# Two transformer blocks on one core: four edits inside the layers of the first block

## The chip, the core and the metric

The kernel runs on one core of a Trainium2 chip. A core has five engines with instruction streams of their own: TensorE (PE in the profile; its weight loads are PEld), VectorE (DVE), ScalarE (ACT), GpSimd (POOL) and SyncE (SP). They are ordered among themselves by semaphores alone, and every order in this kernel is written out by hand. SP and ACT issue DMAs, each on a queue of its own; both queues are served by the same 16 DMA engines. The metric is device time in microseconds of one execution. All times below are in microseconds unless marked ns.

## What is computed

The reference runs `first_block` (two layers) and then `second_block` (a feed-forward part, a hybrid mixer, a second feed-forward part, a norm) on a 512 x 1024 activation in f32. The change lies in the two layers. One layer is, cut to what matters:

```
h = rms_norm(x, norm_g) * (1 + scale) + shift          # scale, shift, gate from c @ w_ada
gq, gk, gv, glr, gz, dq, dk, dv, dz = split(h @ w_in)   # glr has 16 columns, the rank
gq, gk, gv = split(silu(causal_conv([gq, gk, gv])))
log_a = log_sigmoid(glr @ w_gk + b_gk) / 16
k_dec = gk * exp(b_end - cumsum(log_a))                 # per chunk of 64 tokens
u[n]  = k_dec[n].T @ gv[n]                              # outer products, 8 chunks
state = a[n] * state + u[n]; o[n] = gq[n] @ state       # 4 heads, 64 x 128 each
o_gla  = rms_norm(o) * gla_norm_g * silu(gz)
o_diff = rms_norm(attention difference) * diff_norm_g * (1 - lam_init) * silu(dz)
x = x + gate * (concat(o_gla, o_diff) @ w_out)
```

## The kernel before

**Weights.** A layer's weights pass through in 18 units of 128 x 2048 (`L_CONV` 4, `L_K` 2, `L_Q` 2, `L_V` 2, `L_Z` 4, `L_OUT` 4). SP loads a unit into `raw` (L460), ACT rounds it to `wh` (L539, `take_high`), GpSimd takes the remainder `wl = raw - wh` (L496). Two buffers alternate, by the parity of the unit. The activation is split alike into `xh` and `xl` (in the output units `mix_h` and `mix_l`), and PE forms each product as three matmuls, `wh*xh`, `wh*xl` and `wl*xh` (L880 to L882, `products`; for token blocks L909 to L911). PE waits for `w_ready` before it starts a unit and for `banks_free` (its PSUM banks have been emptied, or claimed again) before it writes.

**The order inside a layer.** `layer_order` makes one list of stages that all engines follow. The weight units up to z are cut into quarters, `("part", stage, j, p)`, 56 of them, and `put(n, stage)` places a smaller piece of work behind quarter n. The pieces which the change touches: `lr` (n = 3), the 16 rank columns `glr`, as 8 `products` of 128 x 512; `gate` (n = 6), `glr @ w_gk + b_gk`, in which a row of ones in `glr` carries the bias; `outer` (n = 25 to 32), the outer product of one chunk of 64 tokens per call. PE makes the outer products (L1113), DVE turns them into `states` (L1647 and L1649), and `read_out` (n = 27, 29, 31, 33; L1128) multiplies by the states. A chunk's 64 tokens lie on partitions 0 to 63 or 64 to 127, by its parity, and its outer product goes to PSUM bank 4 or 5.

**The last z unit and the first two output units.** When PE has finished the last quarter of z, ACT's list is: a root and a Silu of earlier z columns, then `take_high` for the second output unit (L539), then the Silu of the last z bank out of PSUM (L645), which releases `banks_free`. PE's list is: `claim` and `chunk_ready` for both output units, then `first_out(0, 0)` and `first_out(0, 1)` (24 matmuls of 128 x 512 with the GLA half), `turn_output(4)` and `(5)` (L1056), `first_out(1, 0)`, `turn_output(6)` and `(7)`, `first_out(1, 1)`.

**The start.** SP issues x, eight 1 MB tiles of `w_ada` and two weight units. ACT makes the squares of x and then issues the small loads (`small_loads`, L513 to L523), and only behind those stands the root for the first norm (L596). DVE turns the root into a diagonal (L1383, L1384), PE spreads it (L1001), and behind that on PE stand the `w_ada` tiles 2 to 7 (L968), whose sums give the scale and shift that the first matmuls' input needs. `o_g` holds the four output norm weights (two layers, two branches) as columns of 128 partitions; DVE multiplies two of them by `1 - lam_init` (L1533).

Of the kernel before, what the change touches and what calls it, by code (L numbers as in the profile page):

```python
# [25 lines left out]
F32 = mybir.dt.float32  # L26
# [5 lines left out]
P = 128  # L32
D = 1024
S = 512
# [43 lines left out]
def layer_order():  # L78
# [24 lines left out]
    for c in range(NCH):  # L103
        put(25 + c, "outer", c)
# [64 lines left out]
def build(nc, ins, out):  # L169
    ctx = ExitStack()  # L170
    with ctx:  # L171
# [56 lines left out]
        o_g = sb("o_g", [P, LAYERS, 2])  # L228
        c_wide = sb("c_wide", [P, KT, 32])
        wgk = sb("wgk", [RANK + 1, LAYERS, GLA_QK])  # L230
        glr = sb("glr", [32, S])
# [49 lines left out]
        wr_h = at("wr_h", [P, KT, P], F32R, at_p)  # L281
        wr_l = at("wr_l", [P, KT, P], F32R, at_p + 4096)
# [80 lines left out]
        glr_copied = sem("glr_copied")  # L363
        conv_done = sem("conv_done")
# [80 lines left out]
        N_SMALL = 16 * (len(small) + 3 + LAYERS)  # L445
# [63 lines left out]
        def _(act):  # L509

            def small_loads():
# [7 lines left out]
                act.dma_start(o_g[:], ins["o_g"].rearrange("o (l a d) -> (o d) l a", l=LAYERS, a=2), allow_slow_non_contiguous=True  # L519
                              ).then_inc(small_in, 16)  # L520
                act.dma_start(wgk[0:RANK], ins["w_gk"]).then_inc(small_in, 16)
                for l in range(LAYERS):
                    act.dma_start(wgk[RANK:RANK + 1, l], ins["b_gk"][l:l + 1]).then_inc(small_in, 16)  # L523
# [101 lines left out]
            for l in range(LAYERS):  # L625
# [3 lines left out]
                def empty(stage, j, t):  # L629
# [4 lines left out]
                    if t:  # L634
                        take_high(unit + 2)
                    bank = ps[:, t]
                    func = ACT.Silu if (stage, j) == ("z", L_Z - 1) else ACT.Copy
# [7 lines left out]
                    nc.scalar.activation(dst, bank, func).then_inc(banks_free[u], 1)  # L645

# [34 lines left out]
                for stage, *at_ in ORDER:  # L681
# [194 lines left out]
        def _(pe):  # L876
# [132 lines left out]
            for l in range(LAYERS):  # L1009
# [125 lines left out]
                for stage, *at_ in ORDER:  # L1135
# [14 lines left out]
                    elif stage == "lr":  # L1150

                        pe.wait_ge(lr_w, l + 1)
                        for k in range(KT):
                            last = products(ps[:, 4], (wr_h[:, k], wr_l[:, k]), (xh[:, k], xl[:, k]),
                                            k == 0, k == KT - 1)
                        last.then_inc(glr_done, 1)
                    elif stage == "gate":

                        pe.wait_ge(glr_copied, l + 1)
                        for tb in range(TB):  # L1160
                            last = nc.tensor.matmul(ps[:, 4 + tb // 2, (tb % 2) * 256:(tb % 2) * 256 + 256],
                                                    glr[0:RANK + 1, tb * P:tb * P + P], wgk[:, l],
                                                    start=True, stop=True)
# [86 lines left out]
                turn_output(5)  # L1250
                first_out(1, 0, gla)
# [94 lines left out]
        def _(dve):  # L1346
# [129 lines left out]
            def rank_zeros():  # L1476
                link(nc.vector.memset(wr_h[:].bitcast(F32), 0.0))
                link(nc.vector.memset(wr_l[:].bitcast(F32), 0.0))

            def rank_weights(l):  # L1480

                link(nc.vector.tensor_copy(wr_h[:, :, 0:RANK], wr_raw[:, l]))
                nc.vector.tensor_tensor(wr_l[:, :, 0:RANK], wr_raw[:, l], wr_h[:, :, 0:RANK].bitcast(F32),
# [48 lines left out]
            for l in range(LAYERS):  # L1532
                link(nc.vector.tensor_scalar(o_g[:, l, 1:2], o_g[:, l, 1:2], 1.0 - lam_init(l), None, ALU.mult))  # L1533
            for l in range(LAYERS):
# [68 lines left out]
                for stage, *at_ in ORDER:  # L1603
                    if stage == "ada_turn":
                        if l == 0:
# [7 lines left out]
                            dve.sem_inc(late_mod, 1)  # L1613
                    elif stage == "conv":
# [24 lines left out]
                    elif stage == "outer":  # L1639

                        c = at_[0]
                        dve.wait_ge(outer_done, l * NCH + c + 1)
                        if c:
                            dve.wait_ge(state_ready, l * NCH + c)
                        for p in range(2):
                            if c == 0:
                                ins_ = nc.vector.tensor_copy(states[:, 0, p], ps[:, 4, p * 256:p * 256 + 256])  # L1647
                            else:
                                ins_ = nc.vector.scalar_tensor_tensor(  # L1649
                                    out=states[:, c, p], in0=states[:, c - 1, p], scalar=aend[:, p, c:c + 1],  # L1650
                                    in1=ps[:, 4 + c % 2, p * 256:p * 256 + 256], op0=ALU.mult, op1=ALU.add)
                            if p == 0:
                                link(ins_)
# [268 lines left out]
```

## Time and profile before

| | |
|---|---|
| median of 3 runs | 1887.44 us (1887.17 to 1890.46) |
| profiled execution, its own time | 1887.43 us |
| its span in the trace | 1885.7 us, so 1.73 us lie around it |
| PE busy | 1786.2 us, 95% |
| PEld, DVE, ACT, POOL busy | 78%, 49%, 34%, 35% |
| mean granted TensorE clock | 0.977 |

The profiled execution's time is the median to within 0.01 us, so its trace stands for the runs. PE has work for 95% of the span; what can be taken from the time is PE's own work and the stretches in which PE waits. In a row of a timeline, the first number is the start, the second the time that the merged instructions took, and the bracket is the idle time ahead of them with what ended it.

### The profile page before, as it was taken

How to read it: one execution, taken by the hardware profiler on the slowest of the kernel's cores; microseconds unless marked ns; L12 is line 12 of the kernel's file. 1: busy time of each engine (PE TensorE's matmuls, PEld its weight loads, DVE VectorE, ACT ScalarE, POOL GpSimd, SP SyncE). 2: the span in 40 equal slices, each digit the busy share in tenths (PEclk: the TensorE clock that was granted, in tenths of full speed). 3: DMA queues.
4: the chain of work that ended last, by engine and by line, in shares of the span. 5: the costliest groups of instructions: out<-in, count | busy, mean ns of one | idle time of the engine just before them, and what ended most of it. 6: DMA issues, size and time to landing. Idle time of an engine off the chain costs nothing.

```text
span 1885.7 us, 22633 instructions
## 1 busy us (share of the span) xinstructions
PE 1786.2 (95%) x9032; PEld 1467.1 (78%) x9032; DVE 924.2 (49%) x888; ACT 639.9 (34%) x785; POOL 661.0 (35%) x163
## 2 busy tenths in 40 slices
PE   3999997899998999999998999899999999999997
PEld 1677896678887778888886988778888878888885
DVE  3654655766475545555223136663223645555223
ACT  3332463343355343333223332222222343333221
POOL 2222122233112244344344244424434344343442
PEclk9999998899998999999998999999999999999998
DMA  8562111212111122322223232312222222222221
GB/s 321 187 236 95 65 46 45 89 61 74 68 46 68 68 89 89 103 97 75 92 92 102 85 111 89 112 45 90 99 101 89 90 89 93 108 89 89 80 94 71
DMA packets 30145, 180.71 MB, mean 96 GB/s; under 512 B 4850, under 2 KB 4980, under 8 KB 12548
## 3 DMA queue, kind: packets, MB, share of 16 engines
q1 hardware_dynamic: 24480, 161.50, 24.3%
q10 hardware_dynamic: 5604, 18.36, 2.7%
q8 instruction: 44, 0.72, 0.2%
q14 instruction: 17, 0.14, 0.0%
HBM read 177.74 MB, written 2.10 MB: 95 GB/s over the span
## 4 chain that ended last, share of the span: by engine, by line
issue 66%; PE 18%; POOL 14%; POOLq 0%; DVE 0%; ACT 0%; DVEq 0%; ACTq 0%
POOL wl L496 14%; PE ps L882 6%; PE ps L880 6%; PE ps L881 6%; DVE y L1396 0%; POOLq L501 0%; PE ps L1001 0%; POOLq L495 0%; ACT L596 0%; PE ps L994 0%; DVE sq L1384 0%; DVEq L171 0%; ACT sq L568 0%; POOL glr L484 0%; ACTq L171 0%
## 5 line engine op out<-in xcount | busy, mean ns | idle before, releaser
L496 POOL TENSOR_TENSOR wl<-raw,wh 128x2048 fp32r<-128x2048 f32 (+1 forms) x152 | 659.0, 4336 | 1197.7 <-ACT wh L539 1197.7
L880 PE MATMUL ps<-xh,wh 128*128 128x512 f32 x1280 | 504.5, 394 | 12.6 <-DVE xl L1359 5.6
L881 PE MATMUL ps<-xl,wh 128*128 128x512 f32 x1280 | 500.4, 391 | 0.0
L882 PE MATMUL ps<-xh,wl 128*128 128x512 f32 x1280 | 500.1, 391 | 0.0
L539 ACT ACTIVATE wh<-raw 128x2048 fp32r<-128x2048 f32 x152 | 291.0, 1915 | 524.0 <-PE ps L882 483.2
L880 PEld LDWEIGHTS ps<-xh,wh 128*128 128x128 f32 x1280 | 241.7, 189 | 75.6 <-issue 24.0
L882 PEld LDWEIGHTS ps<-xh,wl 128*128 128x128 f32 x1280 | 241.5, 189 | 51.0
L881 PEld LDWEIGHTS ps<-xl,wh 128*128 128x128 f32 x1280 | 241.8, 189 | 49.6
L1747 DVE TENSOR_TENSOR fl<-tmp,fh 128x512 f32 x44 | 194.9, 4430 | 84.7 <-ACT fh L792 84.7
L909 PE MATMUL ps<-wh,xh 128*128 128x256 f32 x608 | 178.9, 294 | 0.0
L910 PE MATMUL ps<-wh,xl 128*128 128x256 f32 x608 | 173.1, 285 | 0.0
L911 PE MATMUL ps<-wl,xh 128*128 128x256 f32 x608 | 173.0, 285 | 0.0
L882 PE MATMUL ps<-fh,wl 128*128 128x512 f32 x352 | 140.4, 399 | 0.0
L881 PE MATMUL ps<-fl,wh 128*128 128x512 f32 x352 | 138.7, 394 | 0.0
L880 PE MATMUL ps<-fh,wh 128*128 128x512 f32 x352 | 138.0, 392 | 0.0
L909 PEld LDWEIGHTS ps<-wh,xh 128*128 128x128 f32 x608 | 117.7, 194 | 18.4 <-issue 17.4
L910 PEld LDWEIGHTS ps<-wh,xl 128*128 128x128 f32 x608 | 117.8, 194 | 0.0
L911 PEld LDWEIGHTS ps<-wl,xh 128*128 128x128 f32 x608 | 117.5, 193 | 0.0
L1373 DVE TENSOR_TENSOR sumsq<-sumsq,sq 128x512 f32<-128x512 f32 x36 | 87.8, 2438 | 37.4 <-ACT sq L568 36.7
L1742 DVE TENSOR_TENSOR tmp<-ps,gate 128x512 f32<-128x512 f32 x44 | 30.4, 692 | 134.1 <-PE ps L882 131.8
L784 ACT ACTIVATE gate<-gate 128x512 f32<-128x512 f32 x44 | 27.9, 633 | 195.8 <-DVE gate L1737 195.8
L1434 DVE TENSOR_TENSOR gate<-ps,r_bc 128x512 f32<-128x512 f32 x16 | 11.1, 691 | 154.6 <-PE ps L882 154.6
(241 smaller groups left out, 2128.8 us busy)
## 6 DMA issues: line engine op xcount, KB each, us to landing
raw<-ffn_in_stream SPq DMA_DIRECT2D x44, 1024.0 KB, 4.8
raw<-mixer_stream SPq DMA_DIRECT2D x40, 1024.0 KB, 4.8
raw<-layer_stream SPq DMA_DIRECT2D x36, 1024.0 KB, 4.9
raw<-ffn_out_stream SPq DMA_DIRECT2D x32, 704.0 KB, 4.1
ada_w<-w_ada SPq DMA_DIRECT2D x8, 1024.0 KB, 18.6
ada_late<-w_ada ACTq DMA_DIRECT2D x16, 512.0 KB, 4.7
ada_late<-w_ada ACTq DMA_DIRECT2D x8, 1024.0 KB, 7.4
x<-x_t SPq DMA_DIRECT2D x1, 2048.0 KB, 7.8
```

Source lines behind the costliest of these rows:

```text
L496: nc.gpsimd.tensor_tensor(wl[u][:, 0:size], raw[u][:, 0:size], wh[u][:, 0:size].bitcast(F32), ALU.subtract).then_inc(w_ready, 1)
L539: nc.scalar.activation(wh[u][:], raw[u][:], ACT.Copy).then_inc(w_high, 1)
L784: nc.scalar.activation(gate[:, u], gate[:, u], ACT.Silu).then_inc(ff_gate, 1)
L880: nc.tensor.matmul(bank_ap, w0, x0, start=first, stop=False)
L881: nc.tensor.matmul(bank_ap, w0, x1, start=False, stop=False)
L882: return nc.tensor.matmul(bank_ap, w1, x0, start=False, stop=last)
L909: nc.tensor.matmul(dst, xh[:, k, cols], wh[u][:, w], start=(k == 0), stop=False)
L910: nc.tensor.matmul(dst, xl[:, k, cols], wh[u][:, w], start=False, stop=False)
L911: last = nc.tensor.matmul(dst, xh[:, k, cols], wl[u][:, w], start=False, stop=(k == KT - 1))
L1373: ins_ = nc.vector.tensor_tensor(sumsq[:], sumsq[:], sq[:, m % 2], ALU.add)
L1742: nc.vector.tensor_tensor(tmp[:, u], ps[:, 2 * u + 1], gate[:, u], ALU.mult).then_inc(tmp_ready, 1)
L1747: nc.vector.tensor_tensor(fl[:, bass.ds(i * 2 + u, 1)], tmp[:, u:u + 1], fh[:, bass.ds(i * 2 + u, 1)].bitcast(F32), ALU.subtract).then_inc ...
```

## The change

It does four things. (1) The output norm weights are loaded as four rows of 128 elements (`o_rows`) instead of element by element into 128 partitions; once, behind the first layer's `lr`, PE turns them and DVE copies them into `o_g` and scales them; PE's `gate` waits for this (`og_ready`). (2) PE awaits the second output unit behind `turn_output(5)`, no longer at the first matmul, and on ACT the last z bank is emptied ahead of `take_high`. (3) The outer products come two chunks per call, `("outer", tb)` at n = 25, 27, 29, 31, with the row halves alternating. (4) High and low halves of the rank columns lie side by side in one tile `wr` (columns 0 to 15 and 16 to 31), so that two matmuls replace three; the high and low sums come out as 32 rows of `glr` and are added by the gate's contraction, for which `w_gk` is loaded twice.

```diff
-    for c in range(NCH):
-        put(25 + c, "outer", c)
+    for tb in range(TB):
+        put(25 + 2 * tb, "outer", tb)
...
-                act.dma_start(o_g[:], ins["o_g"].rearrange("o (l a d) -> (o d) l a", l=LAYERS, a=2), allow_slow_non_contiguous=True
+                act.dma_start(o_rows[:], ins["o_g"].rearrange("o (r d) -> (o r) d", r=2 * LAYERS)
                               ).then_inc(small_in, 16)
-                act.dma_start(wgk[0:RANK], ins["w_gk"]).then_inc(small_in, 16)
+                for half in range(2):
+                    act.dma_start(wgk[half * RANK:(half + 1) * RANK], ins["w_gk"]).then_inc(small_in, 16)
...
-                    if t:
+                    last = (stage, j) == ("z", L_Z - 1)
+                    if t and not last:
                         take_high(unit + 2)
...
                     nc.scalar.activation(dst, bank, func).then_inc(banks_free[u], 1)
+                    if t and last:
+                        take_high(unit + 2)
...
-                        nc.scalar.activation(glr[0:RANK], ps[0:RANK, 4], ACT.Copy).then_inc(glr_copied, 1)
+                        nc.scalar.activation(glr[0:2 * RANK], ps[0:2 * RANK, 4], ACT.Copy).then_inc(glr_copied, 1)
...
-                def outer(c):
-                    if c >= 2:
-                        pe.wait_ge(state_ready, l * NCH + c - 1)
-                    rows = slice(64 * (c % 2), 64 * (c % 2) + 64)
+                def outer(tb):
+                    if tb:
+                        pe.wait_ge(state_ready, l * NCH + 2 * tb)
                     for p in range(2):
-                        last = nc.tensor.matmul(ps[:, 4 + c % 2, p * 256:p * 256 + 256],
-                                                decay[rows, c // 2, p * P:p * P + P],
-                                                gv[rows, c // 2, p * 256:p * 256 + 256],
-                                                start=True, stop=True)
-                    last.then_inc(outer_done, 1)
+                        for half in range(2):
+                            rows = slice(64 * half, 64 * half + 64)
+                            last = nc.tensor.matmul(ps[:, 4 + half, p * 256:p * 256 + 256],
+                                                    decay[rows, tb, p * P:p * P + P],
+                                                    gv[rows, tb, p * 256:p * 256 + 256],
+                                                    start=True, stop=True)
+                            if p:
+                                last.then_inc(outer_done, 1)
...
                         for k in range(KT):
-                            last = products(ps[:, 4], (wr_h[:, k], wr_l[:, k]), (xh[:, k], xl[:, k]),
-                                            k == 0, k == KT - 1)
+                            nc.tensor.matmul(ps[:, 4], wr[:, k], xh[:, k], start=(k == 0), stop=False)
+                            last = nc.tensor.matmul(ps[:, 4], wr[:, k], xl[:, k], start=False, stop=(k == KT - 1))
                         last.then_inc(glr_done, 1)
+                        if l == 0:
+                            pe.wait_ge(small_in, N_SMALL)
+                            nc.tensor.transpose(ps[:, 5, 0:2 * LAYERS], o_rows[:], ident[0:2 * LAYERS, 0:2 * LAYERS]
+                                                ).then_inc(og_turned, 1)
...
                 for u in range(2):
                     claim(0, out_unit, u)
-                    chunk_ready(0, out_unit, u)
+                chunk_ready(0, out_unit, 0)
...
                 turn_output(5)
+                chunk_ready(0, out_unit, 1)
                 first_out(1, 0, gla)
...
-                link(nc.vector.memset(wr_h[:].bitcast(F32), 0.0))
-                link(nc.vector.memset(wr_l[:].bitcast(F32), 0.0))
+                link(nc.vector.memset(wr[:].bitcast(F32), 0.0))
```

On DVE the stage `outer` now updates two chunks' states behind one wait for `outer_done`, and the two scalings of `o_g` move from the start into the first layer's `lr` stage, with a copy ahead of them.

Three places in the order. First, on ACT around the last z bank of the first layer, before the change:

```order
L764 ACT_TABLE_LOAD
L764 ACTIVATE sd_o_119<-ss_o_118,eps_63 128x16 [waits o_var]
L761 ACT_TABLE_LOAD
L761 ACTIVATE zg_105<-zg_105 128x4x256 [waits banks_free0]
L539 ACTIVATE wh1_55<-raw1_53 128x2048 [waits raw_landed1,tile_done]
L645 ACTIVATE zg_105<-ps 128x2x256
```

and with it:

```order
L770 ACT_TABLE_LOAD
L770 ACTIVATE sd_o_120<-ss_o_119,eps_63 128x16 [waits o_var]
L767 ACT_TABLE_LOAD
L767 ACTIVATE zg_106<-zg_106 128x4x256 [waits banks_free0]
L649 ACTIVATE zg_106<-ps 128x2x256 [waits tile_done]
L542 ACTIVATE wh1_55<-raw1_53 128x2048 [waits raw_landed1]
```

The last two have changed places; nothing ahead of them moved. Second, on PE at the output units of the first layer with the change (`wh_55` belongs to the second output unit; before the change its `w_ready` was awaited by the first of these rows, which already names that semaphore for the first unit, and the row below the transposes had no wait):

```order
L886 MATMUL ps<-mix_h_132,wh_54 128x512 [waits banks_free1,w_ready,banks_free0,mix_low]
...
L888 MATMUL ps<-mix_h_132,wl_56 128x512
L1062 MATMUL ps<-ident,o_diff 128x128 [waits o_normed]
L1062 MATMUL ps<-ident,o_diff 128x128 x3
L1062 MATMUL ps<-ident,o_diff 128x128 [waits o_normed]
L1062 MATMUL ps<-ident,o_diff 128x128 x3
L886 MATMUL ps<-mix_h_132,wh_55 128x512 [waits w_ready]
```

The wait for the second unit now stands behind 24 matmuls and two output transposes. Third, on PE at the outer products of the first layer, first before the change:

```order
L1113 MATMUL ps<-gv,decay 128x256 [waits gv_ready,gk_ready]
L1113 MATMUL ps<-gv,decay 128x256
...
L1113 MATMUL ps<-gv,decay 128x256 x2
...
L1113 MATMUL ps<-gv,decay 128x256 [waits state_ready]
L1113 MATMUL ps<-gv,decay 128x256
L1128 MATMUL ps<-states,conv 64x128 [waits state_ready]
```

and with it:

```order
L1120 MATMUL ps<-gv,decay 128x256 [waits gv_ready,gk_ready]
L1120 MATMUL ps<-gv,decay 128x256 x3
...
L1120 MATMUL ps<-gv,decay 128x256 [waits state_ready]
L1120 MATMUL ps<-gv,decay 128x256 x3
L1136 MATMUL ps<-states,conv 64x128 [waits state_ready]
```

Two calls of two matmuls, a quarter apart, have become one call of four; the call that a `read_out` follows now waits for the states of both chunks of the call before it.

## Rows read from the trace of the kernel before

**Rows 1.** The page: busy time of each engine, share of the span, instructions.

```profile
PE 1786.2 (95%) x9032; PEld 1467.1 (78%) x9032; DVE 924.2 (49%) x888; ACT 639.9 (34%) x785; POOL 661.0 (35%) x163
```

**Rows 2.** PE's waits over the span: total, times, longest.

```profile
PE ps L880 <- POOL wl L496: 23.1, 6, 8.6
PE ps L1001 <- DVE sq L1384: 20.9, 4, 12.7
```

**Rows 3.** Timeline of ACT at the start, its DMA issues among it.

```profile
18.71 1.96 ACTq L519 DMA_DIRECT2D o_g<-o_g  x1
20.70 9.11 ACTq L521 DMA_DIRECT2D wgk<-w_gk  x1
29.84 0.80 ACTq L523 DMA_DIRECT2D wgk<-b_gk  x2
30.67 1.28 ACT L596 ACT_TABLE_LOAD   x1 [15.67 <-issue]
```

**Rows 4.** Timeline of PE at the start.

```profile
33.33 2.07 PE L1001 MATMUL ps<-sq,ones 128*128 128x512 f32 x2 [12.71 <-DVE sq L1384]
35.33 6.07 PE L968 MATMUL ps<-ada_w,c_wide 128*32 128x512 f32 x48
45.19 0.47 PE L880 MATMUL ps<-xh,wh 128*128 128x512 f32 x1 [2.40 <-DVE xl L1497]
```

**Rows 5.** GB/s in 40 slices of 0 to 70 us (1.75 us each).

```profile
GB/s 0 162 393 421 384 426 426 426 431 431 414 401 411 408 406 410 409 416 414 300 8 0 75 337 187 150 431 28 0 5 0 0 0 0 0 2 255 421 426 428
```

**Rows 6.** Timeline of PE: the rank columns of the first layer, and the next wait.

```profile
56.18 0.50 PE L880 MATMUL ps<-xh,wr_h 128*128 128x512 f32 x1
...
61.79 0.39 PE L880 MATMUL ps<-xh,wh 128*128 128x512 f32 x1
...
66.95 1.40 PE L981 MATMUL ps<-ada_late,c_wide 128*32 128x512 f32 x8 [2.28 <-DMA ada_late<-w_ada]
```

**Rows 7.** Timeline of ACT behind the last z quarter, first layer.

```profile
296.20 1.89 ACT L539 ACTIVATE wh<-raw 128x2048 fp32r<-128x2048 f32 x1
298.00 0.58 ACT L645 ACTIVATE zg<-ps 128x512 f32<-128x512 f32 x1
```

**Rows 8.** Timeline of GpSimd there.

```profile
298.17 4.62 POOL L496 TENSOR_TENSOR wl<-raw,wh 128x2048 fp32r<-128x2048 f32 x1 [12.35 <-ACT wh L539]
```

**Rows 9.** Timeline of PE there, and the same place in the second layer.

```profile
294.02 0.28 PE L911 MATMUL ps<-wl,xh 128*128 128x256 f32 x1
302.93 0.77 PE L880 MATMUL ps<-mix_h,wh 128*128 128x512 f32 x1 [8.64 <-POOL wl L496]
...
310.22 1.03 PE L1056 MATMUL ps<-ident,o_diff 128*128 128x128 f32 x8
311.01 0.48 PE L880 MATMUL ps<-mix_h,wh 128*128 128x512 f32 x1
...
606.05 0.77 PE L880 MATMUL ps<-mix_h,wh 128*128 128x512 f32 x1 [8.64 <-POOL wl L496]
```

**Rows 10.** A stretch there: busy time of PE, PEld, DVE, ACT, POOL, then PEclk.

```profile
302.90:307.20 4.30, 4.27 (x12) 3.39 (x13) 1.04 (x2) 0.00 (x0) 0.00 (x0) 0.58 0.74 244
```

**Rows 11.** Timeline of PE around one outer product and one score, before and behind each.

```profile
152.13 0.39 PE L882 MATMUL ps<-xh,wl 128*128 128x512 f32 x1
152.45 1.13 PE L1113 MATMUL ps<-gv,decay 64*128 64x256 f32 x4
153.51 0.50 PE L880 MATMUL ps<-xh,wh 128*128 128x512 f32 x1
...
245.20 0.70 PE L1081 MATMUL ps<-kf,q 64*128 64x256 f32 x4
245.83 0.39 PE L909 MATMUL ps<-wh,xh 128*128 128x256 f32 x1
```

**Rows 12.** Timeline of DVE at the outer products of the second layer.

```profile
452.36 5.24 DVE L1674 TENSOR_TENSOR k_sq<-k_tok 128x1024 f32<-128x1024 f32 x1 [5.47 <-ACT k_tok L645]
461.38 1.00 DVE L1649 SCALAR_TENSOR_TENSOR states<-states,aend,ps 128x256 f32<-128x256 f32 x2 [1.49 <-PE ps L1113]
```

More of the change, by code:

```diff
@@ L228, in build @@
         o_g = sb("o_g", [P, LAYERS, 2])
+        o_rows = sb("o_rows", [2 * LAYERS, P])
         c_wide = sb("c_wide", [P, KT, 32])
-        wgk = sb("wgk", [RANK + 1, LAYERS, GLA_QK])
-        glr = sb("glr", [32, S])
+        wgk = sb("wgk", [2 * RANK + 1, LAYERS, GLA_QK])
+        glr = sb("glr", [2 * RANK + 1, S])
         wr_raw = sb("wr_raw", [P, LAYERS, KT, RANK])
@@ L363, in build @@
         glr_copied = sem("glr_copied")
+        og_turned = sem("og_turned")
+        og_ready = sem("og_ready")
         conv_done = sem("conv_done")
@@ L444, in build @@
         ]
-        N_SMALL = 16 * (len(small) + 3 + LAYERS)
+        N_SMALL = 16 * (len(small) + 4 + LAYERS)
         @block.sync
@@ L633, in empty @@
                     act.wait_ge(tile_done, 2 * unit + t + 1)
-                    if t:
+                    last = (stage, j) == ("z", L_Z - 1)
+                    if t and not last:
                         take_high(unit + 2)
                     bank = ps[:, t]
-                    func = ACT.Silu if (stage, j) == ("z", L_Z - 1) else ACT.Copy
+                    func = ACT.Silu if last else ACT.Copy
                     if stage == "conv":
@@ L1153, in _ @@
                         for k in range(KT):
-                            last = products(ps[:, 4], (wr_h[:, k], wr_l[:, k]), (xh[:, k], xl[:, k]),
-                                            k == 0, k == KT - 1)
+                            nc.tensor.matmul(ps[:, 4], wr[:, k], xh[:, k], start=(k == 0), stop=False)
+                            last = nc.tensor.matmul(ps[:, 4], wr[:, k], xl[:, k], start=False, stop=(k == KT - 1))
                         last.then_inc(glr_done, 1)
+                        if l == 0:
+                            pe.wait_ge(small_in, N_SMALL)
+                            nc.tensor.transpose(ps[:, 5, 0:2 * LAYERS], o_rows[:], ident[0:2 * LAYERS, 0:2 * LAYERS]
+                                                ).then_inc(og_turned, 1)
                     elif stage == "gate":
                         pe.wait_ge(glr_copied, l + 1)
+                        pe.wait_ge(og_ready, 1)
                         for tb in range(TB):
                             last = nc.tensor.matmul(ps[:, 4 + tb // 2, (tb % 2) * 256:(tb % 2) * 256 + 256],
-                                                    glr[0:RANK + 1, tb * P:tb * P + P], wgk[:, l],
+                                                    glr[:, tb * P:tb * P + P], wgk[:, l],
                                                     start=True, stop=True)
@@ L1531, in _ @@
             nc.vector.tensor_reduce(lam_s[:], lam_p[:], AX_X, ALU.add).then_inc(lam_ready, 1)
-            for l in range(LAYERS):
-                link(nc.vector.tensor_scalar(o_g[:, l, 1:2], o_g[:, l, 1:2], 1.0 - lam_init(l), None, ALU.mult))
             for l in range(LAYERS):
@@ L1613, in _ @@
                             dve.sem_inc(late_mod, 1)
+                    elif stage == "lr":
+                        if l == 0:
+                            dve.wait_ge(og_turned, 1)
+                            link(nc.vector.tensor_copy(o_g[:].rearrange("p l a -> p (l a)"), ps[:, 5, 0:2 * LAYERS]))
+                            for ll in range(LAYERS):
+                                link(nc.vector.tensor_scalar(o_g[:, ll, 1:2], o_g[:, ll, 1:2], 1.0 - lam_init(ll),
+                                                             None, ALU.mult))
+                            dve.sem_inc(og_ready, 1)
                     elif stage == "conv":
@@ L1639, in _ @@
                     elif stage == "outer":
[L1641 to L1653, printed above, removed]
-                        ins_.then_inc(state_ready, 1)
+                        for c in (2 * at_[0], 2 * at_[0] + 1):
+                            dve.wait_ge(outer_done, l * NCH + 2 * at_[0] + 2)
+                            if c:
+                                dve.wait_ge(state_ready, l * NCH + c)
+                            for p in range(2):
+                                if c == 0:
+                                    ins_ = nc.vector.tensor_copy(states[:, 0, p], ps[:, 4, p * 256:p * 256 + 256])
+                                else:
+                                    ins_ = nc.vector.scalar_tensor_tensor(
+                                        out=states[:, c, p], in0=states[:, c - 1, p], scalar=aend[:, p, c:c + 1],
+                                        in1=ps[:, 4 + c % 2, p * 256:p * 256 + 256], op0=ALU.mult, op1=ALU.add)
+                                if p == 0:
+                                    link(ins_)
+                            ins_.then_inc(state_ready, 1)
                     elif stage == "gla_ss":
```

10 lines of the change are left out of this document (5 added, 5 removed).

## The prediction

> **What bounds the kernel now.** I read the page first: PE is busy for 95% of the span and no other engine for more than half of it [rows 1]. So the time can fall in two ways only, by less work on PE or by shorter waits of PE. Then the list of PE's waits: the largest is for GpSimd's `wl` (23.1 in 6 waits, 8.6 the longest), the next for the norm's diagonal (20.9 in 4, 12.7 the longest) [rows 2]. Last I read the timelines around these waits and around PE's small instructions in the layers. The reader is to see that each of the four edits touches PE's work or one of its two largest waits.
>
> **The start.** ACT issues `o_g` at 18.71 and the load behind it takes 9.11 to issue, where two later ones take 0.80 together; the norm's root stands behind these and starts at 30.67 [rows 3]. Through the root and the diagonal PE's spread begins at 33.33, 2.66 later, and behind it six `w_ada` tiles take 6.07 and end at 41.40; the first product starts at 45.19, 3.79 after that [rows 4]. All that time the DMA engines move over 400 GB/s for SP, until some 34.5 (the slice from 33.25 shows 300, the next one 8) [rows 5]. Each earlier small load has one row per partition, 128 in all; `o_g` has four single elements per partition, 512. My reading: ACT's queue is slow because SP's transfers share the engines, and it is the 512 pieces that fill it, so the next issue must wait. With four rows in their place I let the new load cost as much as `o_g` did (1.96, to 20.67) and the four behind it 0.40 each with a little waiting: ACT is free at 22.5, not 30.67. PE's spread then begins at 25.2 and ends at 27.3, tiles 2 to 7 could be done 6.07 later, at 33.3, but the last lands at 34.5 only and takes 1.0 (at half the clock 2.0): done at 35.5 to 36.5, and the first product at 39.3 to 40.3. The gain is 5.9 to 4.9; I take 5.2, since PE has been busy less densely by then and may start the products at the lower clock. What is late next is the `w_ada` load itself, so no more can come from here.
>
> [...]
>
> **The rank columns.** 24 matmuls take 61.79 - 56.18 = 5.61, 0.234 each, with PE at work before and after [rows 6]. Eight fewer are 1.87 per layer, 3.7 in all. The gate's contraction has 33 rows and no more columns, at one price. The transpose of `o_rows`, the smallest kind of instruction, stands ahead of a wait of 2.28 for `ada_late` [rows 6], whose load is issued behind the same `glr`; the wait covers it. Were it bare it would cost some 0.3. DVE's copy and two scalings (an estimate of 0.6 at most, as three small operations) fall where DVE waits for PE's `gate`; one `memset` fewer is as hidden. I count these at nothing.
>
> **The output units.** PE ends z at 294.3 and waits until 302.93, in the second layer the same 8.64 [rows 9]. It waits for `wl` of the second output unit: ACT casts from 296.20 to 298.09, empties the last z bank until 298.58 [rows 7], GpSimd takes 4.62 from 298.17 [rows 8]. In the new order ACT empties the bank at 296.20 (0.58), which gives PE its second claim at 296.8; the first unit's `wl` has long been there. PE starts at 296.95, 6.0 sooner. ACT's cast moves back by 0.5, so `wl` of the second unit is ready at 298.7 + 4.62, with the handover 303.5. PE now reaches it behind 24 matmuls and two transposes, which took 311.01 - 302.93 = 8.08 before [rows 9], with the clock at 0.58 for most of the stretch [rows 10]. At full clock the 24 take 24 x 0.234 = 5.6 and the whole 6.4. So PE is at the second unit at 303.5 (full clock, both there at once) or 305.0 (clock as before), and was there at 311.01: 7.5 or 6.0 per layer. After an idle time of 2.28 the matmuls of rows 6 also ran some microseconds slower, so I stay near the lower end: 6.5 per layer, 13.0 in all. DVE's gating of the last two token blocks may be held by GpSimd until 304; PE wants these two transposes after 306. The third output unit's `wl` hangs on PE's own end of the first, so it moves along.
>
> **The outer products.** One call of two matmuls begins 0.32 behind the last product's start, and the next product starts at 153.51; without the call it would be 0.234 behind: the call costs 153.51 - 152.13 - 0.23 = 1.15 [rows 11]. Its two matmuls share one row half. The scores show the other case: two matmuls of 256 columns on the two row halves take 245.83 - 245.20 = 0.63 together [rows 11], where the two of the outer call take 153.51 - 152.45 = 1.06. The halves run side by side. A new call holds two such pairs: 1.06 to 1.26 plus 0.09 for the switch, against 2.30 for two old calls. I take 1.15, since the second pair's weights can be loaded under the first, as in the old call: 4 calls x 1.15 saved per layer, 9.2 in all. With 1.35 it is 7.6; if nothing overlaps only the switches go, 0.7. The wait for the states is longer by one chunk, but the call stands two quarters (over 5) behind its predecessor, and DVE's pair of updates takes 1.00 [rows 12]. In the second layer DVE came late to the first states (its `k_sq` took 5.24) and still had the second chunk's at 462.4, while the new second call would stand at about 463. It fits by little; a wait of 1 or so there is inside the range.
>
> The Trainium skill, page "TensorE: Matmul & The Clock Gate", section "Part 3: Packing small matmuls", warns that semaphore increments of tiles completing together serialize, 26.3 ns each; the call now has two. An estimate by that page is 0.2 for all eight calls, and no row here shows it apart.
>
> **The sum.** 5.2 + 3.7 + 13.0 + 9.2 = 31.1. The profiled execution's own time is 1887.43, its span 1885.7 with 1.73 around it, and the median of the runs 1887.44, so I subtract from that: 1856.3.
>
> **The rivals.**
> - *The row halves do not overlap in the new call* (each matmul waits for the one before it, as the old ones do). For it: pairs behind pairs are not in the trace. Against it: rows 11. Gain 0.7 in place of 9.2: 1864.8. Chance 0.09.
> - *ACT is held at the start all the same*, by the nine loads ahead or by the extra one for `w_gk`. [...] Gain 0 in place of 5.2: 1861.5. Chance 0.10.
> - *The wait for the output unit moves instead of shrinking*: PE stands at the second unit, or ACT's list of roots and Silu is later than I think, so that 4 per layer remain of the 6.5. 1861.3. Chance 0.05.
> - *Slower: DVE's state updates come late behind GpSimd.* `k_sq` took 5.24, while GpSimd was at its 4.6 (compare 1.00 for two updates [rows 12]), so a hold is worth 4. The new calls and the read-outs wait for states at 14 places in the two layers. If eight of them were held by 4, the 31 would be gone; below that the change still gains. Against it: the updates read PSUM and took 1.00 in every row, and GpSimd is at work for one 4.6 in some 15 there. Chance 0.03, at 1890 to 1900. The Trainium skill, page "SBUF — State Buffer", section "Who interferes with whom", has the rule for such holds: DVE with two SBUF inputs blocks while GpSimd holds the shared ports. By that rule the updates, with one input in PSUM, go free, and the rival falls.
> - *The change does nothing that shows*: 0.01.
>
> My forecast keeps 0.72.
>
> **How the numbers follow.** The bounds of the terms: start 3.2 (with products started at half the clock, 1.7) to 5.9, rank 3.7, output 12.0 to 15.0, outer products 7.6 to 9.9: 26.5 to 34.5, or 1861 to 1853. Waits elsewhere may shift the clock's lower stretches by a few microseconds either way. So the range reaches from 1850.5 to the first rival, 1864.5. A measurement of this kernel tells about 0.2%, 3.8, from no change. Every case but the fourth and the last lies far below that: faster 0.96, same 0.01, slower 0.03.
>
> **What would show it.** In the new trace ACT's root should start near 22.5, PE's spread near 25, the first product near 40; the rank columns should take 16 matmuls per layer, not 24; the wait ahead of the first output product should be 2.6, with none or under 1 at the second unit; a call of eight outer records should take about 1.1. A root still near 30, or outer calls of 2.1, would make the prediction wrong by that term; so would a new wait of PE for `states`.

## The result and the profile after

The changed kernel takes 1855.66 us (median of 4 runs, 1850.46 to 1856.5), the kernel before 1887.31 in the same session: ratio 0.9821, 95% interval 0.9808 to 0.9833. That is 31.65 less, where 31.1 was forecast. The profiled execution took 1855.71, its span is 1854.0.

The page of the changed kernel, engines' busy time:

```profile
PE 1772.8 (96%) x9017; PEld 1458.5 (79%) x9017; DVE 936.6 (51%) x887; ACT 640.4 (35%) x785; POOL 661.7 (36%) x163
```

Against [rows 1], PE is busy for 13.4 less; the other 18 of the 31.7 that the span lost were waits. PE's largest waits after the change (total, times, longest):

```profile
PE ps L974 <- DMA ada_w<-w_ada: 14.0, 3, 11.8
PE ps L1007 <- DVE sq L1398: 12.6, 4, 4.3
...
PE ps L886 <- POOL wl L498: 5.8, 4, 1.8
...
PE ps L886 <- ACT zg L649: 5.5, 2, 2.7
```

Against [rows 2], the wait for `wl` fell from 23.1 to 5.8 (the two of 8.6 are gone, two of 2.7 for `zg` have come), that for the norm's diagonal from 20.9 to 12.6. The one for the `w_ada` tiles rose, from 11.6 to 14.0: PE is now early enough to wait for the last of them. PE waits for `states` nowhere.

ACT at the start, changed kernel:

```profile
18.81 1.54 ACTq L521 DMA_DIRECT2D o_rows<-o_g  x1
20.38 0.81 ACTq L524 DMA_DIRECT2D wgk<-w_gk  x2
21.22 1.09 ACTq L526 DMA_DIRECT2D wgk<-b_gk  x2
22.34 1.28 ACT L599 ACT_TABLE_LOAD   x1 [7.30 <-issue]
```

The issue of 9.11 of [rows 3] is gone and the root's table load starts 8.33 sooner. PE there:

```profile
25.00 2.07 PE L1007 MATMUL ps<-sq,ones 128*128 128x512 f32 x2 [4.35 <-DVE sq L1398]
...
34.82 1.06 PE L974 MATMUL ps<-ada_w,c_wide 128*32 128x512 f32 x8 [1.53 <-DMA ada_w<-w_ada]
...
39.66 0.77 PE L886 MATMUL ps<-xh,wh 128*128 128x512 f32 x1 [2.40 <-DVE xl L1511]
...
62.30 1.06 PE L987 MATMUL ps<-ada_late,c_wide 128*32 128x512 f32 x8 [1.86 <-DMA ada_late<-w_ada]
```

The first product stands 5.53 ahead of its place in [rows 4], but the wait for `ada_late` only 4.65 ahead of [rows 6], although 8 matmuls are gone in between. The stretches of PE show why (busy time of PE, PEld, DVE, ACT, POOL, then PEclk):

```profile
39.60:46.50 6.90, 6.84 (x18) 5.39 (x19) 6.72 (x12) 5.28 (x7) 0.00 (x0) 0.55 0.13 53
46.50:62.00 15.50, 13.95 (x61) 10.93 (x59) 11.39 (x21) 3.80 (x5) 4.60 (x1) 1.00 0.23 77
```

The first products ran at 0.55 of the full clock for 6.9, which is nearly the lower level of 1.2 GHz. That gave 2.9 back: the first rank matmul stands at 53.52 against 56.18 [rows 6], only 2.66 ahead. Part of it returned behind the wait for `ada_late`, where the kernel before had run at the lower clock and the changed one did not (the kernel before first, columns as above):

```profile
68.20:71.00 2.80, 2.80 (x11) 2.15 (x8) 0.00 (x0) 0.00 (x0) 0.00 (x0) 0.51 1.03 430
```

```profile
63.30:66.20 2.90, 2.90 (x16) 2.17 (x12) 0.98 (x2) 0.00 (x0) 0.00 (x0) 1.00 1.03 428
```

At the next `ada_late` matmuls PE is 6.23 ahead (66.24 against 72.47), 1.6 more than at the wait. An outer call and the output units of the first layer, PE, with the second layer's first unit:

```profile
145.89 0.39 PE L888 MATMUL ps<-xh,wl 128*128 128x512 f32 x1
146.21 1.13 PE L1120 MATMUL ps<-gv,decay 64*128 64x256 f32 x8
147.27 0.50 PE L886 MATMUL ps<-xh,wh 128*128 128x512 f32 x1
...
283.20 0.28 PE L917 MATMUL ps<-wl,xh 128*128 128x256 f32 x1
286.22 0.48 PE L886 MATMUL ps<-mix_h,wh 128*128 128x512 f32 x1 [2.73 <-ACT zg L649]
...
291.90 1.03 PE L1062 MATMUL ps<-ident,o_diff 128*128 128x128 f32 x8
292.75 0.50 PE L886 MATMUL ps<-mix_h,wh 128*128 128x512 f32 x1
...
575.02 0.76 PE L886 MATMUL ps<-mix_h,wh 128*128 128x512 f32 x1 [2.73 <-ACT zg L649]
```

A call holds eight records now, where [rows 11] has four, and lasts as long: 147.27 - 146.21 = 1.06, as 153.51 - 152.45. So do the seven other calls. The wait ahead of the output unit is 2.73 in place of 8.64 [rows 9], and no wait stands at the second unit. It only just fits in the first layer. GpSimd's `wl` of the second unit:

```profile
287.85 4.85 POOL L498 TENSOR_TENSOR wl<-raw,wh 128x2048 fp32r<-128x2048 f32 x1 [12.83 <-ACT wh L542]
```

It is ready at 292.70, and PE comes to it at 292.75. A PE that came earlier would wait there, so this place has no more to give unless ACT or GpSimd gets faster.

### The profile page after: what moved, and what is told of

Same layout as the page of the kernel before. It is cut to its first block, busy times and chain, and to the rows that moved or that the text cites. A ratio compares the mean times of both kernels' runs of the same rounds, so it can differ in the third digit from the quotient of the medians.

```text
span 1854.0 us, 22604 instructions
## 1 busy us (share of the span) xinstructions
PE 1772.8 (96%) x9017; PEld 1458.5 (79%) x9017; DVE 936.6 (51%) x887; ACT 640.4 (35%) x785; POOL 661.7 (36%) x163
## 4 chain that ended last, share of the span: by engine, by line
issue 66%; PE 19%; POOL 14%; POOLq 0%; DVE 0%; ACT 0%; DVEq 0%; ACTq 0%
POOL wl L498 14%; PE ps L888 6%; PE ps L887 6%; PE ps L886 6%; DVE y L1410 0%; POOLq L503 0%; PE ps L1007 0%; POOLq L497 0%; ACT L599 0%; PE ps L1000 0%; DVE sq L1398 0%; DVEq L171 0%; ACT sq L571 0%; POOL glr L486 0%; ACTq L171 0%
## 5 line engine op out<-in xcount | busy, mean ns | idle before, releaser
L886 PE MATMUL ps<-xh,wh 128*128 128x512 f32 x1280 | 504.8, 394 | 12.6 <-DVE xl L1373 5.6
```

The source lines that it names most:

```text
L886: nc.tensor.matmul(bank_ap, w0, x0, start=first, stop=False)
```

## The experiments

Every run was compared with the kernel before on the same chip (median there 1887.29 for the first four, 1888.1 for the next four, 1888.47 for the last four).

**The four parts alone.** First `e1_start`, the kernel before with:

```
-                act.dma_start(o_g[:], ins["o_g"].rearrange("o (l a d) -> (o d) l a", ...
+                act.dma_start(o_rows[:], ins["o_g"].rearrange("o (r d) -> (o r) d", r=2 * LAYERS)
...
+                            nc.tensor.transpose(ps[:, 5, 0:2 * LAYERS], o_rows[:], ident[...])
```

> The kernel before with the first part alone: the output norm weights loaded as rows (o_rows) and turned by PE. My theory (ACT is held by the 512 pieces of o_g): ACT is free for its roots at about 22, PE's spread begins near 25, the first product stands near 39.7 in place of 45.19 and the time falls by 5.2 to 5.6, to 1882.0. The rival (ACT is held by the number of loads or by SP's traffic, whatever o_g looks like): the root stays near 30 and the time at 1887.4.

Measured: 1882.71 (8 runs, 1880.39 to 1883.53), ratio 0.9973 (0.9962 to 0.9983), 4.6 less. Spread at 23.99, first product at 39.71. As expected, a little smaller.

`e2_outer`, with the new `outer(tb)` and DVE's double update alone:

```
-                    rows = slice(64 * (c % 2), 64 * (c % 2) + 64)
...
+                        for half in range(2):
+                            rows = slice(64 * half, 64 * half + 64)
```

> The kernel before with the outer products in row pairs alone. My theory (the two row halves run side by side): a call of eight records costs about 1.1, as an old call of four did, so 4 x 1.15 = 4.6 per layer and 9.2 in all: 1878.2. The rival (no overlap, only the switches are saved): a call of 2.1 and a gain of 0.7, 1886.7. A second rival: PE comes to wait for the states, each such wait being visible ahead of an outer call.

Measured: 1879.04 (6 runs), ratio 0.9953 (0.994 to 0.9966), 8.3 less. A call of eight records takes 157.29 - 156.23 = 1.06, and PE waits for no state. A part was lost at places that have nothing to do with the calls: in its profile PE is 3.8 late at 76.25 (72.47 before), 1.2 of it from the `w_ada` tiles, about as much from a lower clock at the first products, and 1.27 from a wait for `ada_late` there. Stretches at the lower clock that were shorter later on gave much of that back.

`e3_out`, with PE's later wait and ACT's swap alone:

```
-                    chunk_ready(0, out_unit, u)
+                chunk_ready(0, out_unit, 0)
...
+                chunk_ready(0, out_unit, 1)
...
+                    if t and last:
+                        take_high(unit + 2)
```

> The kernel before with the later wait for the second output unit and ACT's swapped order alone. My theory: the wait ahead of the first output product falls from 8.64 to about 2.7, none stands at the second unit, and the gain is 6.0 to 7.5 per layer: 13 to 14 in all, 1874. Rival (the wait moves to the second unit): 4 per layer, 8 in all, 1879.4.

Measured: 1873.95 (6 runs), ratio 0.9929 (0.9911 to 0.9947), 13.3 less. The wait ahead of the first unit is 2.73, and none stands at the second.

`e4_rank`, with the rank halves in one tile alone:

```
-                            last = products(ps[:, 4], (wr_h[:, k], wr_l[:, k]), (xh[:, k], xl[:, k]), ...
+                            nc.tensor.matmul(ps[:, 4], wr[:, k], xh[:, k], start=(k == 0), stop=False)
+                            last = nc.tensor.matmul(ps[:, 4], wr[:, k], xl[:, k], start=False, ...
```

> The kernel before with the two halves of the rank weight in one tile alone, with o_g loaded element by element as before and w_gk loaded twice behind it. My theory: 8 matmuls fewer per layer at 0.234 each, 3.7 in all; the second w_gk load adds some 0.8 to ACT's hold at the start, so 1883.7 to 1884.5. Rival (the wait for ada_late behind it takes it back): in the first layer the shorter block only lengthens that wait of 2.28, and the gain is 1.9 or less, 1885.5.

Measured: 1881.71 (6 runs), ratio 0.9963 (0.995 to 0.9976), 5.6 less, more than either theory gave. The timeline of ACT in `e4_rank` shows that the start did get worse, by the second load behind `o_g`:

```profile
18.96 1.75 ACTq L518 DMA_DIRECT2D o_g<-o_g  x1
20.75 9.73 ACTq L521 DMA_DIRECT2D wgk<-w_gk  x2
```

Its first product stands at 47.08, 1.89 later than before: 0.67 is the later root, and 1.2 are 48 tile matmuls that took 7.30 in place of 6.07 [rows 4], for which I found no cause: the profile shows the full clock there. The rank columns gave 1.94 and 1.82 in the two layers. The rest came at places that the edit doesn't touch: 1.7 between 403 and 511 (times of the kernel before), and 2.2 between 1022 and 1511, where the lower stretches of the clock were shorter in this run. The four parts alone sum to 4.6 + 8.3 + 13.3 + 5.6 = 31.8; all together gave 31.65. That they add up so well is partly luck, since `e4_rank` has a loss at the start that the whole change doesn't have, and a gain from the clock.

**Why ACT was held.** `e5_og_last` is the kernel before with the element-wise load moved behind the others:

```
-                act.dma_start(o_g[:], ins["o_g"].rearrange(...)).then_inc(small_in, 16)
                 act.dma_start(wgk[0:RANK], ins["w_gk"]).then_inc(small_in, 16)
                 for l in range(LAYERS):
                     act.dma_start(wgk[RANK:RANK + 1, l], ins["b_gk"][l:l + 1]).then_inc(small_in, 16)
+                act.dma_start(o_g[:], ins["o_g"].rearrange(...)).then_inc(small_in, 16)
```

> The kernel before with the element-wise o_g load moved behind the w_gk and b_gk loads, nothing else changed. My theory (it is the 512 pieces that fill ACT's queue, and only the issue behind them has to wait): with nothing behind it, o_g holds ACT for about 2 only, the table load starts near 23, the spread near 25, the first product near 40 and the time is that of the start part alone, 1882. The rival (the queue is slow at that time whatever stands in it, or the w_gk load itself is dear): some load issue still takes 9, the table load stays near 30 and the time at 1887.4.

Measured: 1882.04 (7 runs), ratio 0.9969 (0.9958 to 0.998), which can't be told from `e1_start`. ACT's timeline in `e5_og_last`:

```profile
18.86 1.95 ACTq L519 DMA_DIRECT2D wgk<-w_gk  x1
20.84 0.80 ACTq L521 DMA_DIRECT2D wgk<-b_gk  x2
21.67 0.40 ACTq L522 DMA_DIRECT2D o_g<-o_g  x1
22.10 1.28 ACT L596 ACT_TABLE_LOAD   x1 [6.96 <-issue]
```

The same 512 pieces take 0.40 to issue when they come last, and `w_gk` in the place where `o_g` stood takes its 1.95. So neither load is dear in itself. The tenth load of the list takes 1.5 to 2.0, whatever it is, and the one behind the 512 pieces takes 9. The edit's form (rows and a transpose) isn't needed for this gain; moving one load to the end of the list gives it. Whether the number of the pieces makes the 9, or that each is a single element, no run separates.

**What the swap on ACT carries.** `e6_wait_only` is the kernel before with the two lines of `chunk_ready` moved and ACT's order left:

> The kernel before with PE's later wait for the second output unit alone; ACT still casts that unit ahead of emptying the last z bank. My theory: PE then waits for the emptied bank (zg, begun behind the cast at 298.1) until about 298.7, so its wait is 4.4 in place of 8.64, and it reaches the second unit later than the wl of 303 or so: 4.2 per layer if the clock stays as it was, up to 6 if it rises: 8.5 to 12 in all, 1875.5 to 1879. The rival (the swap of ACT's order carries nothing): the gain is that of the whole output part, 13.3, and the wait ahead of the first unit is 2.7.

Measured: 1879.73 (6 runs, of which one of 4547.65, far off every other of any kernel, tells nothing; the other five lie between 1877.17 and 1882.26, with a median of 1878.54), ratio 0.9956 (0.9943 to 0.997), 8 to 10 less. PE, then ACT, in `e6_wait_only`:

```profile
299.88 0.47 PE L880 MATMUL ps<-mix_h,wh 128*128 128x512 f32 x1 [4.53 <-ACT zg L645]
```

```profile
297.25 1.89 ACT L539 ACTIVATE wh<-raw 128x2048 fp32r<-128x2048 f32 x1
299.05 0.58 ACT L645 ACTIVATE zg<-ps 128x512 f32<-128x512 f32 x1
```

The traces tell the two parts better than the medians. From the last z product to the second output unit PE takes 16.99 and 17.32 in the two layers of the kernel before, 12.83 and 12.80 here, and 9.54 and 11.04 in `e3_out`. So the later wait carries 8.7 of 13.7, and the swap, which costs ACT and GpSimd nothing that PE sees, the other 5.0.

**Overlap or fewer calls.** `e7_halves` is the changed kernel with the loops exchanged:

```
-                    for p in range(2):
-                        for half in range(2):
+                    for half in range(2):
+                        for p in range(2):
```

> The changed kernel with the two loops of the outer products exchanged: the two products of one row half come behind each other, then those of the other half (same work, same number of calls). My theory (the gain comes from two row halves at work side by side, not from fewer calls): a call of eight records costs more than 1.1: 1.6 if the second of the first half and the first of the other still overlap, 2.1 if none do; 8 calls, so 4 to 8 over the changed kernel: 1859.7 to 1863.5. The rival (the gain is that of fewer switches, whatever the order): the call stays at 1.1 and the time at 1855.7.

Measured: 1852.57 (5 runs, 1851.31 to 1857.78), ratio 0.9816 (0.9802 to 0.9831). PE in `e7_halves`:

```profile
146.96 1.14 PE L1120 MATMUL ps<-gv,decay 64*128 64x256 f32 x8
148.03 0.50 PE L886 MATMUL ps<-xh,wh 128*128 128x512 f32 x1
```

The call takes 1.07: my theory's 1.6 to 2.1 missed, and the order doesn't matter. So this run doesn't tell overlap from a mere count of calls; `e11_same_half` does:

```
-                            rows = slice(64 * half, 64 * half + 64)
+                            rows = slice(0, 64)
```

> The changed kernel with all four products of an outer call on rows 0 to 63: the odd chunks' products are made from the even chunk's rows, so the states and the output are not the reference's; count, shapes and order are those of the changed kernel. With the loops exchanged the call still took 1.07, so order doesn't matter; this run tells overlap from the number of calls. My theory (two row halves at work at once make the gain): nothing can overlap, a call takes about 2.1, and 8 calls cost some 8.5 more: 1864.2. The rival (the gain is that of fewer calls, each call costs 1.1): the call stays at 1.1 and the time at 1855.7.

Measured: 1863.03 (4 runs), ratio 0.9857 (0.9843 to 0.9872); the changed kernel on the same chip took 1854.71 (below), 8.3 less. PE in `e11_same_half`:

```profile
146.82 1.99 PE L1120 MATMUL ps<-gv,decay 64*128 64x256 f32 x8
148.74 0.50 PE L886 MATMUL ps<-xh,wh 128*128 128x512 f32 x1
```

A call of four such products takes 1.92 on one row half and 1.06 on two, so it is the overlap: 0.86 for each of 8 calls, 6.9. The rest of the 9.2, 0.3 for each call, comes from fewer calls: two old ones cost 2 x 1.15, a new one without overlap 1.92 + 0.09.

**The clock and the start.** `e8_filler` is the changed kernel with, among others:

```
+                    def filler(n):
+                        for _ in range(n):
+                            nc.tensor.matmul(ps[:, 2, 0:256], ones[:], x[:, 0, 0:256], start=True, stop=True)
```

> The changed kernel with extra matmuls (ones by x, 256 columns, into a bank that nobody reads; no result uses them) where PE waits ahead of the first products: 1, 2, 1 and 4 of them between the last spreads, the norm's and the first product. In the changed kernel the window from 39.6 to 46.5 shows PEclk 0.55. My theory (the clock falls because PE has been idle in the waits from 32 to 39.6): the first products run at full clock and the time falls by up to 3.4, to 1852.5, if the extra matmuls themselves delay nothing. The rival (the clock is low there for another reason, or it is given back at another place): the stretch of about 0.55 stays, or moves, and the time is within 1 of 1855.7.

Measured: 1851.35 (5 runs, 1848.43 to 1855.23), ratio 0.9803 (0.9789 to 0.9818). `e12_after_again` is the changed kernel once more, on the chip of the last four runs:

> The changed kernel itself once more, on the same chip as the three above, so that they can be held against it. Expected: 1855.7 as before, with single runs between 1850.5 and 1857. If its median here is near 1852 or 1853 (as for the kernel with the loops exchanged and the one with the extra matmuls), differences of up to 3 between these kernels are the spread of the clock's low stretches, not the edits.

Measured: 1854.71 (5 runs, 1846.14 to 1856.8), ratio 0.9811 (0.9793 to 0.9829). So the 1851.35 is no proven gain: the two intervals overlap for the most part. Stretches of the changed kernel, of `e8_filler` and of `e12_after_again`, one fence each (columns as above):

```profile
34.90:46.50 11.60, 8.48 (x30) 5.88 (x31) 8.72 (x17) 7.64 (x10) 1.27 (x1) 0.71 0.47 177
...
183.00:197.00 14.00, 14.00 (x95) 12.22 (x95) 4.85 (x6) 5.25 (x7) 3.36 (x1) 0.88 0.01 1
285.00:298.00 13.00, 11.78 (x59) 9.73 (x60) 10.57 (x10) 5.30 (x7) 4.85 (x1) 1.00 0.24 83
```

```profile
34.90:46.50 11.60, 10.85 (x53) 7.90 (x46) 8.83 (x18) 7.65 (x10) 1.03 (x1) 1.00 0.47 179
...
183.00:197.00 14.00, 14.00 (x82) 12.26 (x81) 4.54 (x6) 5.25 (x7) 3.05 (x1) 0.76 0.00 0
285.00:298.00 13.00, 11.50 (x42) 9.27 (x43) 9.77 (x9) 4.31 (x5) 4.79 (x1) 0.74 0.24 83
```

```profile
34.90:46.50 11.60, 8.44 (x27) 5.27 (x28) 7.36 (x15) 7.63 (x10) 1.37 (x1) 0.56 0.48 176
...
183.00:197.00 14.00, 14.00 (x89) 13.11 (x89) 2.67 (x6) 4.72 (x7) 1.18 (x1) 0.76 0.00 1
285.00:298.00 13.00, 10.27 (x40) 8.18 (x39) 9.87 (x9) 5.41 (x6) 4.79 (x1) 0.74 0.17 49
```

The extra matmuls do keep the clock up at the start (1.00 against 0.71), and PE reaches `ada_late` at 59.47, 2.8 sooner. But right behind that wait the clock fell, where the changed kernel has 1.00 (63.30 to 66.20, above). `e8_filler`:

```profile
60.40:64.50 4.10, 4.10 (x15) 3.18 (x12) 0.90 (x2) 0.00 (x0) 0.00 (x0) 0.58 1.03 426
```

At the next `ada_late` matmuls only 1.25 is left (64.99 against 66.24). At 183 the clock fell for longer (0.76 against 0.88) and at 285 it fell where it had not (0.74 against 1.00), and at the last norm 0.77 was left (1839.29 against 1840.06). The unchanged kernel shows the falls at 183 and 285 too in its second profile, without a full clock at the start; and `e10_both` (below) has the full clock at the start and 1.00 at 285. So that fall doesn't follow from the one avoided at the start. Two profiles of the unchanged kernel differ at the start as well: its first product stands at 39.66 in one and at 41.05 in the other.

`e9_raw_late` is the changed kernel with:

```
-                if k in (0, 5):
-                    u = k // 5
+                if k in (0, KT - 1):
+                    u = k // (KT - 1)
```

and ACT's cast of the second unit behind the `xh` casts.

> The changed kernel with the second projection unit's weights loaded behind the last w_ada tile, and ACT's cast of that unit behind the norm's work. My theory (what holds the first product is the arrival of the w_ada tiles, and 1 MB less ahead of them brings it forward by 2.5): first product at about 37.3, time 1853.5 if the later cast stays hidden. The rival (the second unit's wl comes late instead): a wait of PE for wl near 45 takes the 2.4 back: 1855.7 or more.

Measured: 1854.98 (5 runs, 1853.58 to 1855.57), ratio 0.9824 (0.9811 to 0.9837): the same as the changed kernel's 1854.71. The first product did come forward and no wait for `wl` took its place. PE in `e9_raw_late`, two places, then DVE:

```profile
37.59 0.76 PE L886 MATMUL ps<-xh,wh 128*128 128x512 f32 x1 [2.40 <-DVE xl L1511]
...
201.20 0.66 PE L1096 MATMUL ps<-ident,prob 128*128 128x128 f32 x4 [1.39 <-DVE prob L1602]
```

```profile
43.39 4.90 DVE L1529 TENSOR_SCALAR tmp<-xn,mod 128x512 f32<-128x512 f32 x1
```

2.07 sooner at the first product, and 0.05 at 201.20, where the changed kernel stands at 201.25: PEclk was 0.76 between 183 and 197 here, 0.88 there. At the last norm it is 1.03 ahead (1839.03 against 1840.06), which the medians don't show. The rival's wait never showed, but the later `wl` did harm of another kind, which PE hardly saw here: the DVE operation above takes 0.55 elsewhere, and PE waited 0.25 for what follows it.

`e10_both` has both edits:

> The two candidates together: extra matmuls that nobody reads ahead of the first products, and the second unit's weights loaded behind the w_ada tiles. By my theory of the start the first product stands at about 37.3 and the first products run at full clock, but the profile of the run with the extra matmuls alone showed the lower clock again at 183.5 and 285.9, so what the clock gives at the start is largely lost later: some 1852, against 1850.5 if the two gains (2.4 and 2.8) simply added.

Measured: 1857.24 (5 runs, 1853.88 to 1860.31), ratio 0.9839 (0.9826 to 0.9852), rather slower than the changed kernel. PE, then DVE, then GpSimd, in `e10_both`:

```profile
39.22 0.47 PE L886 MATMUL ps<-xh,wh 128*128 128x512 f32 x1 [0.67 <-DVE xl L1521]
...
50.55 0.50 PE L886 MATMUL ps<-xh,wh 128*128 128x512 f32 x1 [2.88 <-DVE xl L1521]
```

```profile
45.03 4.86 DVE L1539 TENSOR_SCALAR tmp<-xn,mod 128x512 f32<-128x512 f32 x1
```

```profile
45.05 4.56 POOL L498 TENSOR_TENSOR wl<-raw,wh 128x2048 fp32r<-128x2048 f32 x1 [14.18 <-ACT wh L542]
```

Two losses that I had not expected: the extra matmuls now stand in front of `w_ada` tiles that have landed, so the first product comes at 39.22 and not at 37.3; and the later `wl` lies beside DVE's work on the last `xl`. A `TENSOR_SCALAR` that takes 0.55 elsewhere took 4.86, and PE waited 2.88 for it. The same hold of 4.90 stands in `e9_raw_late`; PE, at 0.50 of the clock from 37.50 to 42.70, came later there and waited 0.25. At 285 `e10_both` has the full clock (columns as above):

```profile
285.00:298.00 13.00, 11.93 (x59) 9.87 (x60) 10.57 (x10) 5.15 (x7) 4.86 (x1) 1.00 0.23 83
```

No version tried here beats the changed kernel by more than can be measured.

## Why the prediction was right, point by point

- **The start**, forecast 5.2: 5.53 in the trace at the first product, 4.6 and 6.1 in the two runs that had only this gain. That the load by single elements is the cause, and that the wait falls on the next issue, is shown by `e1_start` and `e5_og_last` together; that it fills a queue which SP's traffic slows is a reading that no run tested. The rival that ACT is held all the same fell, except for the 1.54 that the tenth load still pays. What is late next was as forecast the last `w_ada` tile, at 34.82. The lower clock was mis-sized: the bound of 3.2 had 1.7 for it at the first products, and it cost 2.9 there. The term alone would then be 2.66, below its bound. What the sum didn't have is that the lower stretch behind `ada_late` went away, which gave 1.6 back, so that 4.2 is left of the term there. That this held the sum is luck.
- **The rank columns**, forecast 3.7: 1.85 (57.28 - 53.52 = 3.76 in place of 5.61) and 1.82 in the two layers. The small transpose took about 0.25 of PE and was hidden with the copy, as argued: the wait for `ada_late` behind them is 1.86. The gate's matmuls take 1.99 with 33 rows as with 17.
- **The output units**, forecast 13.0 (12.0 to 15.0): 7.44 in the first layer (292.75 - 283.20 = 9.55 in place of 16.99), where PEclk stayed at 1.00, and 6.36 in the second, where the first matmul took 0.76 and the clock was low: 13.8. The two figures lie near the two ends that were worked out (7.5 and 6.0), in one run. They are no bounds, though: in the second profile of the same kernel the first layer takes 12.26 for this stretch, at a clock of 0.50 from 288.30 to 294.10, and gains 4.7 only, and the two layers together 11.2, below the 12.0. `e6_wait_only` shows that 5.0 of the 13.8 is ACT's swap.
- **The outer products**, forecast 9.2 (7.6 to 9.9): the call costs 147.27 - 145.89 - 0.23 = 1.15 with the switch, as taken and as the old one did. A cost of the second semaphore increment (0.2 in the prediction's estimate) doesn't show: old and new calls last 1.06. The rival of no overlap would by `e11_same_half` have gained 0.3 per new call, 2.3 in all, where I had put 0.7.
- **Slower through late states**: no wait for states in any profile. Each of DVE's 32 writes of `states` in the profile took 0.42 to 0.48, as in the kernel before.
- In the sum the four terms measured in the trace are 5.53 + 3.67 + 13.80 + 9.2 = 32.2, and 31.74 was left at the last norm (1840.06 against 1871.80): what lies between the four places, the clock above all, took 0.5 net. That it came so near is partly luck, since single runs of the changed kernel alone lie between 1846.14 and 1856.8. Nor does the time alone tell the forecast from its rivals: the second and third (1861.5 and 1861.3) lie inside the forecast's range, and it is the rows above that rule them out.

## What to carry to other kernels

When an engine that has urgent work also issues loads, look at the durations of the issues: here the dear one was not the load with many small pieces but the load behind it, and moving the former to the end of the list was worth as much as rewriting it. Split a combined wait by which operand is used first, and let the engine that feeds the first user do that piece first. Put matmuls of half height on different row halves into one call, with nothing between them: four took 1.06 here, as long as two on one half; and where PE bounds a kernel, a gain of 2 or 3 at one place may not reach the end, so compare single runs by their clock.

## What the hardware showed that I had not expected

- **The spread of the runs is the clock.** The five runs of `e12_after_again`: 1846.14 at a mean granted clock of 0.987, 1852.13 at 0.982, 1854.71 at 0.981, 1856.73 and 1856.80 at 0.980. That is 10.6 for 0.007, or 1.5 for each 0.001. Compared at 0.980, the changed kernel (1856.73), `e7_halves` (1857.04) and `e11_same_half` (1863.23) differ by 0.3 and 6.5, nearer to the 0 and 6.9 of the traces than their medians; and `e10_both` (1859.33) is 2.6 slower. The clock is listed to 0.001, so such a comparison is good to 1 or so.
- **Row halves run beside each other in either order.** In `e7_halves` both products of the first half stand ahead of those of the second, and the call still takes 1.07. The Trainium skill, page "TensorE: Matmul & The Clock Gate", section "Part 3: Packing small matmuls", says that matmuls start and end strictly in program order. By that rule the third product could begin only beside the second, and an estimate of the call would be 1.06 + 0.43 = 1.5, with 0.43 for one product from the 0.86 that two cost here. The measured 1.07 speaks against it, and the measurement decides.
- **A load of 512 single elements is issued in 0.40 as the last of the list, and the issue behind it takes 9.1 to 9.7** (two loads in the second case), while the DMA engines move over 400 GB/s. How the 9 divides between the pieces and the traffic of the other queue was not tried.
- **A DVE instruction with a single tensor input can be held too**: 4.86 in place of 0.55 in `e10_both`, beside GpSimd's 4.56, and 4.90 in `e9_raw_late`, beside 4.60. In `e10_both` the two start 0.02 apart and end 0.3 apart; which part of the two instructions collides was not tested.
